# Input rows also laid out turned in DRAM: the first product's stationary rows split from the turned copy

## The reference, cut to what matters

```
x: (1, 256, 2048)
a    = rms_norm(x, attn_norm)        # x * rsqrt(mean(x^2) + 1e-6) * attn_norm
proj = a @ w_in                      # (256, 2048) @ (2048, 2368)
c_q, c_kv, k_rope, q_s, k_s, v_s = split(proj)
... two attentions, w_out, MLP; second block: mixer, cross attention, MLP; final norm
```

## Time and profile before

| what | us |
|---|---|
| median of 3 runs (2603.5 to 2604.96) | 2603.79 |
| the profiled execution, its own time | 2605.14 |
| its span, first to last instruction | 2603.3 |
| PE busy in the span | 2571.5 (99%) |
| first matmul of half 0 starts at | 8.78 |
| half 9 starts at (behind `bias_rest`) | 38.75 |

### The profile page before, as it was taken

How to read it: one execution, slowest core, us unless ns; L and a number is a source line. 1 busy time by engine, 2 the same in 40 slices (tenths; PEclk the granted TensorE clock), 3 DMA queues, 4 the chain that set the end, 5 groups by cost and what they waited for, 6 DMA issues and landing times. The chain is left out here.

```text
span 2603.3 us, 32857 instructions
## 1 busy us (share of the span) xinstructions
PE 2571.5 (99%) x13270; PEld 2178.5 (84%) x13270; DVE 1653.4 (64%) x2061; ACT 1375.0 (53%) x1999; POOL 0.2 (0%) x4
## 2 busy tenths in 40 slices
PE   9999999999999999999999999999999999999998
PEld 7878888888888888887888888888888888888887
DVE  7686566655655567568788866544566555655556
ACT  6565554444444446668878745544444444444444
POOL 0000000000000000000000000000000000000000
PEclk9999999999999999999999999999999999999999
DMA  6534666566666655555454437544565566556554
GB/s 225 164 128 146 212 198 196 189 191 194 194 194 189 190 190 176 191 180 165 146 172 145 146 117 247 169 155 141 183 206 188 188 194 194 194 190 190 190 191 145
DMA packets 235534, 468.78 MB, mean 180 GB/s; under 512 B 8219, under 2 KB 17654, under 8 KB 234102
## 3 DMA queue, kind: packets, MB, share of 16 engines
q1 hardware_dynamic: 234246, 465.11, 55.2%
q10 hardware_dynamic: 1136, 1.58, 0.2%
HBM read 460.36 MB, written 6.29 MB: 179 GB/s over the span
## 5 line engine op out<-in xcount | busy, mean ns | idle before, releaser
L2525 DVE TENSOR_TENSOR WL<-Wt,WH 128x1024 fp32r<-128x1024 f32 (+1 forms) x861 | 1037.8, 1210 | 728.4 <-ACT WH L1805 672.9
L1805 ACT ACTIVATE WH<-Wt 128x1024 fp32r<-128x1024 f32 (+1 forms) x861 | 895.0, 1046 | 772.2 <-PE ps L1191 500.7
L1189 PE MATMUL ps<-WH,XT 128*128 128x512 f32 (+1 forms) x1184 | 470.3, 397 | 1.6 <-DVE XT L2536 1.3
L1189 PE MATMUL ps<-WH,HT 128*128 128x512 f32 (+2 forms) x1176 | 457.3, 389 | 3.3 <-DVE WL L2525 3.3
L1191 PE MATMUL ps<-WH,XT 128*128 128x512 f32 (+1 forms) x1184 | 459.5, 388 | 0.0
L1190 PE MATMUL ps<-WL,XT 128*128 128x512 f32 (+1 forms) x1184 | 458.8, 388 | 0.0
L1191 PE MATMUL ps<-WH,HT 128*128 128x512 f32 (+2 forms) x1176 | 451.6, 384 | 0.0
L1190 PE MATMUL ps<-WL,HT 128*128 128x512 f32 (+2 forms) x1176 | 451.1, 384 | 0.0
L1228 PE MATMUL ps<-XT,WH 128*128 128x512 f32 x960 | 336.5, 394 | 0.0
L1228 PE MATMUL ps<-HT,WH 128*128 128x512 f32 x960 | 336.5, 394 | 0.0
L1227 PE MATMUL ps<-XT,WL 128*128 128x256 f32 x960 | 266.6, 278 | 0.0
(11 more groups left out here) (392 smaller groups left out, 1960.8 us busy)
## 6 DMA issues: line engine op xcount, KB each, us to landing
Wt<-in_mlp_w SPq DMA_DIRECT2D x128, 1024.0 KB, 5.2
Wt<-in_w_up SPq DMA_DIRECT2D x64, 1024.0 KB, 5.5
Wt<-in_w_down SPq DMA_DIRECT2D x64, 1024.0 KB, 5.0
Wt<-in_w_in SPq DMA_DIRECT2D x53, 1024.0 KB, 5.2
Wt<-in_w_out SPq DMA_DIRECT2D x32, 1024.0 KB, 5.1
Wt<-in_xa_wk SPq DMA_DIRECT2D x16, 1024.0 KB, 5.1
Wt<-in_xa_wv SPq DMA_DIRECT2D x16, 1024.0 KB, 5.1
Wt<-in_xa_wq SPq DMA_DIRECT2D x16, 1024.0 KB, 5.2
```

What stands on the lines that cost most here:

```text
L1189: pe.matmul(o, xh, wh, start=start, stop=False)
L1805: act.activation(m.WH[:, i % NR, 0:2 * w], m.Wt[:, slot % NW, h * 2 * w:(h + 1) * 2 * w], ACT.Copy).then_inc(*up("wsplit.a", i))
L2525: dve.tensor_tensor(m.WL[:, i % NR, 0:2 * w], m.Wt[:, slot % NW, h * 2 * w:(h + 1) * 2 * w], m.WH[:, i % NR, 0:2 * w].bitcast(F32), SUB).t ...
```

## The change

`x` is passed a second time, turned on the host into (128, 16, 256). ACT loads this copy into a new tile `XTR` in four DMAs (2, 2, 4 and 8 kt), and `first_rows` makes high and low parts of `XT` from it: ACT scales straight from `XTR`, DVE subtracts. The 32 transposes of x are gone from PE, with the two warm-up matmuls between them. Plain `x` is still needed for the squares: SP loads its four chunks, each behind the next half slot of weights, from `wfirst01` on. A generator `gen_first` emits pairs 2 to 7, one a step; from pair 4 on each step has the squares of one chunk behind it.

```diff
+        self.XTR = arena("XTR", [P, KT, 256], 35328)
...
-    turn_in = chain(*(norm_chunk(p, "ln1", c) for c in range(4)))
     p.do("split_first", 0)
     p.split = 1
-    next(turn_in)
-    p.do("warm", 2, *p.banks(1))
+    p.do("first_rows", 0)
     p.do("split_first", 1)
     p.split_to(1)
-    next(turn_in)
-    p.bg.append(turn_in)
+    p.do("first_rows", 1)
...
+    def gen_first():
+        for pr in range(2, 8):
+            p.do("first_rows", pr)
...
+            if pr > 3:
+                p.do("norm_squares", "ln1", pr - 4)
+            if pr < 7:
+                yield
+        yield
+        p.do("norm_scale", "ln1")
+        p.now("ln1", "scale")
+        yield
...
+    return (f"ld_xt{(0, 1, 2, 2, 4, 4, 4, 4)[pr]}",)
...
-        act.dma_start(m.H[:, :, 0:256], x[:, :, 0:256]).then_inc(*dma("ld_x0a"))
+        act.dma_start(m.XTR[:, 0:2, :], xt[:, 0:2, :]).then_inc(*dma("ld_xt0"))
         act.dma_start(m.GRA[:, :], m.A["attn_norm"].rearrange("(k p) -> k p", p=P)).then_inc(*dma("ld_gain0"))
-        act.dma_start(m.H[:, :, 256:512], x[:, :, 256:512]).then_inc(*dma("ld_x0b"))
-        act.dma_start(m.H[:, :, 512:1024], x[:, :, 512:1024]).then_inc(*dma("ld_x1"))
+        for pr, n in ((1, 2), (2, 4), (4, 8)):
+            act.dma_start(m.XTR[:, 2 * pr:2 * pr + n, :], xt[:, 2 * pr:2 * pr + n, :]).then_inc(*dma(f"ld_xt{pr}"))
...
+    def first_rows(pr):
+        on.wait_ge(*at(*first_sig(pr)))
+        on.wait_ge(*at("prep.v", "gain0"))
+        for kt in (2 * pr, 2 * pr + 1):
+            act.activation(m.turned("ln1", 0, kt), m.XTR[:, kt, :], ACT.Copy, scale=m.g1("attn_norm", kt)).then_inc(
+                *up("ln1.a", "high", kt))
...
+    def first_rows(pr):
+        for kt in (2 * pr, 2 * pr + 1):
+            on.wait_ge(*at("ln1.a", "high", kt))
+            dve.scalar_tensor_tensor(m.turned("ln1", 1, kt), m.XTR[:, kt, :], m.g1("attn_norm", kt),
+                                     m.turned("ln1", 0, kt).bitcast(F32), MUL, SUB).then_inc(*up("ln1.v", "done", kt))
...
-            if slot:
-                a = 1024 + 512 * (slot - 1)
-                sp.dma_start(m.H[:, :, a:a + 512], x[:, :, a:a + 512]).then_inc(*dma(f"ld_x{slot + 1}"))
             for h in range(slot == 0, 2):
                 sp.dma_start(dst[:, 2 * h:2 * h + 2, :], src[:, 2 * h:2 * h + 2, :]).then_inc(*dma(f"wfirst{slot}{h}"))
+                c = 2 * slot + h - 1
+                if c < 4:
+                    sp.dma_start(m.H[:, :, 512 * c:512 * c + 512], x[:, :, 512 * c:512 * c + 512]).then_inc(
+                        *dma(f"ld_x{c}"))
...
+    arrays["in_xt"] = np.ascontiguousarray(arrays["in_x"].reshape(2 * P, KT, P).transpose(2, 1, 0))
```

More of the change, by code:

```diff
@@ L570, in plan_all @@
     p.do("warm", 2, *p.banks(1))
-    turn_in = chain(*(norm_chunk(p, "ln1", c) for c in range(4)))
     p.do("split_first", 0)
     p.split = 1
-    next(turn_in)
-    p.do("warm", 2, *p.banks(1))
+    p.do("first_rows", 0)
     p.do("split_first", 1)
     p.split_to(1)
-    next(turn_in)
-    p.bg.append(turn_in)
+    p.do("first_rows", 1)
+    p.now("ln1", 0)
+    p.now("ln1", 1)
+    p.now("ln1", 2)
+    p.now("ln1", 3)
+    def gen_first():
+        for pr in range(2, 8):
+            p.do("first_rows", pr)
+            p.now("ln1", 2 * pr)
+            p.now("ln1", 2 * pr + 1)
+            if pr > 3:
[6 more added lines that the diff above has]
+        yield
+    p.bg.append(gen_first())
     def gen_prep():
@@ L1121, in rows_sig, with first_sig @@
     return f"hid{tag}.v", "low", int(key[3]), kt // 2
+def first_sig(pr):
+    return (f"ld_xt{(0, 1, 2, 2, 4, 4, 4, 4)[pr]}",)
 def normed_sigs(nm, c, tb):
     if nm == "ln1":
-        return [("ld_x0a",), ("ld_x0b",)] if c == 0 else [(f"ld_x{c}",)]
+        return [(f"ld_x{c}",)]
     if nm in ("ln_c0", "ln_c1"):
@@ L1237, in norm_turn @@
         for tb in range(2):
-            for s in [("ld_x0a",), ("ld_x0b",)][pr:pr + 1] if (nm, c) == ("ln1", 0) else normed_sigs(nm, c, tb):
+            for s in normed_sigs(nm, c, tb):
                 on.wait_ge(*at(*s))
@@ L1784, in begin @@
     def begin():
-        x = m.A["x"].rearrange("a (b p) n -> p (a b) n", p=P)
-        act.dma_start(m.H[:, :, 0:256], x[:, :, 0:256]).then_inc(*dma("ld_x0a"))
+        xt = m.A["xt"]
+        act.dma_start(m.XTR[:, 0:2, :], xt[:, 0:2, :]).then_inc(*dma("ld_xt0"))
         act.dma_start(m.GRA[:, :], m.A["attn_norm"].rearrange("(k p) -> k p", p=P)).then_inc(*dma("ld_gain0"))
-        act.dma_start(m.H[:, :, 256:512], x[:, :, 256:512]).then_inc(*dma("ld_x0b"))
-        act.dma_start(m.H[:, :, 512:1024], x[:, :, 512:1024]).then_inc(*dma("ld_x1"))
+        for pr, n in ((1, 2), (2, 4), (4, 8)):
+            act.dma_start(m.XTR[:, 2 * pr:2 * pr + n, :], xt[:, 2 * pr:2 * pr + n, :]).then_inc(*dma(f"ld_xt{pr}"))
         act.preload_act_table_set(TABLE)
@@ L1813, in norm_turn @@
             on.wait_ge(*at("gemm.t", "end", "m1d7"))
-        on.wait_ge(*at("prep.v", "gain0" if nm == "ln1" else "columns"))
+        on.wait_ge(*at("prep.v", "columns"))
         for kt in (k0, k0 + 1):
@@ L1818, in norm_turn @@
         M.empties(b, nm + ".a")
+    @named
+    def first_rows(pr):
[4 more added lines that the diff above has]
+                *up("ln1.a", "high", kt))
     @named
```

## The result

The changed kernel took 2609.81 us (median of 14 runs, 2608.11 to 2611.65) against 2605.00 us for the kernel before in the same session (14 runs, 2603.41 to 2605.80): a ratio of 1.0021, with a 95% interval of 1.0014 to 1.0029. It is slower by 4.8 us by the medians, against a forecast of +2.9 us, and lies 0.8 us above the upper end of the range (2609.0). The kernel before was itself 1.2 us slower beside these runs than the 2603.79 that the forecast started from; counted from 2605.00, the forecast is 2607.9 and its range reaches to 2610.2. So that the time lies outside the stated range owes as much to this shift of the kernel before as to the error in the difference, 1.9 us. The profiled execution took 2611.45 us with a span of 2609.7, so 6.31 us more than the profiled execution of before (2605.14).

What follows compares the result with a forecast made beforehand. PE, busy 99%, bounds the kernel, its start also short of DMA bandwidth; none of the at most 6.0 us removed was counted, and ACT's lateness of 2.9 us made 2603.8 + 2.9 = 2606.7, range 2602.3 to 2609.0.

Steps and rivals of the forecast that it cites:

- The count of bytes: First product: 5208 KB up to wfirst11, as before for wfirst21 (18.0), less 0.6 us; half 2 at 20.3 against 16.93.
- that rule: Start: each DMA engine drains one whole packet before switching queues; half 1 near 14.85, before half 2 can start either way.
- that ACT and not PE sets half 9: End of first product: bias_rest on PE waits for DVE's cast behind ACT's split 9; half 9 2.9 us later, PE's own lateness 2.0.
- The chain of 6.13 us from split 9 to the cast: Ahead of bias_rest: waits through row scale, copies, split 10 and eviction put DVE's cast 6.13 us behind split 9, at 41.15.
- ACT is 2.9 us late: Halves 4 to 9: splits 6 to 9 follow wfirst21's 22.8 at 3.04 us plus 0.02 handover; split 9 at 35.0 against 32.14.
- The 0.6 us won by larger pieces: Start loads: without x's 1 KB pieces the queues move 392 GB/s, not 305; at most 0.8 us won, 0.6 taken.
- the term that was put at nothing: ACT in the first product: reading XTR in SBUF rather than PSUM costs nothing, at most +-0.1 us a half.
- From there on all lists run as before, shifted; PE has no slack with which to catch up: Behind half 9: the 2.9 us delay carries unchanged to the end of the program.
- The sum: Whole kernel: +2.9 us, 2603.8 to 2606.7; ends +2.0 (PE's own lateness alone) and +4.0.
- The loads are hidden: Rival at the start: two extra megabytes cause no delay, wfirst11 stays at 13.9; 2601.4 to 2602.3; chance 0.20 with half hidden.
- The two queues disturb each other: Rival at the start: rate stays near 305 GB/s four microseconds longer, wfirst21 at 24.3; +5.4, 2609.2 us; chance 0.10.
- The clock falls: Rival: PE idles ahead of half 1 or 2, losing 1.7 us; lateness 3.7, 2607.5 us; counted within the forecast (0.68).

Runs made afterwards that it cites:

- a_noplain_warm8: Changed kernel with 8 zero matmuls ahead of each of halves 1 and 2, without the start's plain x loads and the squares; 2606.34 us, ratio 1.0010.
- a_warm8: Changed kernel with 8 warm-up matmuls on zeros in each of PE's two waits, ahead of halves 1 and 2; 2608.28 us, ratio 1.0014.
- b_alloc: Kernel before with the turned copy of x passed as one more input that nothing reads; 2604.72 us, ratio 1.0001.
- a_2k: Changed kernel with the turned copy loaded in eight DMAs of 2 KB pieces instead of 2, 2, 4 and 8 kt; 2610.59 us, ratio 1.0026.
- b_pad80: Kernel before with 80 transposes of 16x16 added to PE's list in the wait near 1471 us; 2607.20 us, ratio 1.0010.
- a_pad32: Changed kernel with 32 transposes of 16x16 added to PE's list in the wait near 1471 us; 2608.30 us, ratio 1.0015.

## Why the prediction was right and wrong

**Right:** half 0 (7.26 forecast, 7.10), `wfirst01` (10.1 to 11.9; 10.91), half 1 (13.0 to 15.5; 13.84). The count of bytes gave 17.4, 20.1 and 22.8 for `wfirst11`, `wfirst20` and `wfirst21`, and the trace has 17.66, 20.36 and 23.07; half 2 was forecast at 20.3 and began at 20.59. The second trace of the same kernel has 18.07, 20.79, 23.49 and 21.00, so the count is good to 0.3 us in one trace and 0.7 in the other. `a_noplain_warm8` confirmed it: 1 MB less, 2.5 us earlier.

The Trainium skill ("DMA: Bandwidth & Descriptors", Queues, rings and completion order) has an engine drain a whole packet of several descriptors before it goes to the next queue. The trace agrees with turns by packet and not by bytes, but not with packets of several pieces: 42 pieces of 8 KB went against 44 of 2 KB in 1 us. Half 1, 14.85 by that rule and 13.0 by equal bytes, began at 13.84 and 14.73 in the two traces of the changed kernel, and as forecast nothing behind depended on it.

**Right:** that ACT and not PE sets half 9, through the cast and `bias_rest`. `a_warm8` took away both falls of the clock at the start, and half 9 moved by 0.07 us. The chain of 6.13 us from split 9 to the cast stayed (35.55 to 41.68).

**Right within what two traces differ by:** "ACT is 2.9 us late" measured 3.42, and 3.84 in the second trace; `b_alloc` shows that the kernel before can itself be 0.6 late there. Two small terms of it were off. The 0.6 us won by larger pieces can't be told from nothing: `wfirst11` was split at 17.66 and 18.07 for an upper bound of 18.0. And a half of ACT's work took 3.12 us and not 3.06 with its handover, four times over. The split is as quick as before (0.95); the two pieces of rows took 0.80 us from `XTR` in SBUF, where they had taken 0.71 from PSUM. So the term that was put at nothing, within 0.1 us a half, was 0.09.

**Wrong:** the sentence "From there on all lists run as before, shifted; PE has no slack with which to catch up". The lists are shifted in time by 3.4 us, but PE's list is also 72 instructions shorter, and so it reaches every packet of instructions at another place. One of these moved from ahead of the `XKB` load into it, which cost 1.23 us of PE's wait and a fall of the clock of 1.6 us: 2.8 us in the profiled execution. The sum had no term for anything behind half 9. With 3.4 at the start, 2.8 there and 0.1 in between it gives 2605.14 + 6.3 = 2611.4, the profiled 2611.45.

By the medians of the unchanged kernel the difference is 4.8 and 6.7 us in two sessions, and 4.0 and 4.2 with the packet moved away. These intervals overlap; the traces and not the medians carry this. The medians do not say either whether every execution pays the 2.8 us in full.

**The rivals.** "The loads are hidden" is out: ACT waited for five loads. "The two queues disturb each other" is out: from 8 to 10 us they moved 426 GB/s together, more than the 392 of the earlier trace rows, and `wfirst21` came at 23.07 and not behind 24.5. "The clock falls" came true twice at the start. Ahead of half 1 it was hidden, as forecast. Behind half 2's start the prediction had priced it above ACT's lateness; here ACT was later still, and the fall was just short of deciding (half 8 ended at 41.8 for 42.03). In `a_2k` it did decide.

## What to carry to other kernels

Before an engine's work is replaced by a second copy in DRAM, count the bytes ahead of each early load: here the count gave the landings within 0.3 to 0.7 us, and each better order of the loads only moved the wait to what then stood last (`cf_dw_w`, plain x, the weights, the bias chain). Follow a lead or a delay along the list of the slowest engine to the next thing that is late, since this and not the stall that vanishes prices the change. And a change in the number of instructions moves each later packet of them against the large loads, so a range that is otherwise tight needs a few microseconds for it.

## What the runs showed of the hardware

- Instructions reach PE by DMA, in packets of 16 KB on q8, 104 in a program with 13234 matmuls and as many weight loads, 105 in `b_pad80`. One some 6 us behind the issue of a 2 MB load made it land after 8.6 to 9.2 us rather than 7.4 to 8.0, in 9 traces against 9, and only the last of sixteen shares was late.
- Two queues with work alternate piece by piece, whatever the size: 42 against 44 pieces moved 0.34 against 0.08 MB.
- A matmul on fp32 zeros of 256 columns is two passes of 0.21 us; a transpose of 16x16 costs PE 0.03 us in a row of 80.
- A fall of the clock can be there in one trace and not in another behind the same wait of PE: behind 1.59 us near 160 us in the changed kernel the granted clock was 0.72 (160 to 166 us), behind 1.60 us in `a_pad32` 1.00. It was worth 1.6 us.
- A copy from PSUM with a scale was quicker than the same from SBUF: 0.71 against 0.80 us for two pieces of 128x256 on ACT.
- SP's seventh issue of 512 KB at the start took 5.04 us, the six ahead of it 0.43 to 0.73, and all that stands behind it on SP waits. That the number of loads outstanding does it fits; no run tested it.

```profile
5.51 5.04 SPq L3497 DMA_DIRECT2D Wt<-in_w_in  x1
```
